# Second attention of a two-layer trunk: one pass over interleaved branches, or two passes with the compressed branch inside the first

## The reference

```python
s = einsum('bqghd,bngd->bghqn', qi, ck) * scale + tab[bucket]      # compressed: 63 keys
p_c = softmax(s) * any_valid
o_c = einsum(p_c, cv);  imp = einsum('bghqn,nm->bgqm', p_c, ov)    # importance of 16 blocks
_, idx = top_k(score(imp), 8)                                      # per group and query
o_s = softmax(q . k_selected + bias, causal) . v_selected          # selected blocks
o_w = softmax(q . k_window + bias, last 512 positions) . v_window  # local window
o = gate0 * o_c + gate1 * o_s + gate2 * o_w
```

## Time and profile before

| | us |
|---|---|
| median of the runs (3) | 2638.21 (2634.61 to 2641.0) |
| profiled execution, first to last instruction | 2632.5 |
| PE busy | 2527.8 (96%) |
| DVE busy | 1782.6 (68%) |
| ACT busy | 1124.6 (43%) |
| POOL busy | 1160.8 (44%) |
| mean granted clock of PE | 0.979 of full |

### The profile page before, as it was taken

How to read it: one execution, slowest core, us unless ns; L and a number is a source line. 1 busy time by engine, 2 the same in 40 slices (tenths; PEclk the granted TensorE clock), 3 DMA queues, 4 the chain that set the end, 5 groups by cost and what they waited for, 6 DMA issues and landing times. The chain is left out here.

```text
span 2632.5 us, 37842 instructions
## 1 busy us (share of the span) xinstructions
PE 2527.8 (96%) x14000; PEld 2051.9 (78%) x14000; DVE 1782.6 (68%) x2832; ACT 1124.6 (43%) x2184; POOL 1160.8 (44%) x883
## 2 busy tenths in 40 slices
PE   8999899999998999999988999999999999999999
PEld 5778667888887778887876788888788888777887
DVE  6544755477677999853049566666646767799993
ACT  4626543253334434323135566666524333433431
POOL 5462666244443444442236444444633444434441
PEclk8999999999999999999987799999999999999999
DMA  4110002224343544230332413122132334354531
GB/s 167 33 48 33 1 1 116 92 84 156 148 160 136 184 163 153 81 128 32 101 111 72 128 53 105 54 53 54 57 125 77 147 135 171 107 208 148 173 128 64
DMA packets 90973, 275.76 MB, mean 105 GB/s; under 512 B 9879, under 2 KB 38935, under 8 KB 76135
## 3 DMA queue, kind: packets, MB, share of 16 engines
q1 hardware_dynamic: 87240, 255.18, 28.3%
q10 hardware_dynamic: 3552, 18.18, 1.8%
HBM read 197.50 MB, written 73.86 MB: 103 GB/s over the span
## 5 line engine op out<-in xcount | busy, mean ns | idle before, releaser
L1560 PE MATMUL ps<-U_hi,RH 128*128 128x512 f32 x912 | 358.3, 393 | 19.1 <-DVE HOB L856 11.6
L1564 PE MATMUL ps<-U_lo,RH 128*128 128x512 f32 x912 | 356.8, 391 | 0.0
L1565 PE MATMUL ps<-U_hi,RL 128*128 128x512 f32 x912 | 356.7, 391 | 0.0
L1027 POOL TENSOR_TENSOR RL<-RAW,RH 128x512 fp32r<-128x512 f32 x112 | 153.5, 1371 | 419.8 <-ACT RH L737 419.8
L737 ACT ACTIVATE RH<-RAW 128x512 fp32r<-128x512 f32 x280 | 175.5, 628 | 282.9 <-PE ps L1565 275.3
L1511 POOL TENSOR_SCALAR PX<-PX,rinv,GATE 128x640 f32<-128x640 f32 (+7 forms) x256 | 197.8, 783 | 209.3 <-DVE rinv L3281 209.3
L1560 PE MATMUL ps<-U_hi,W_hi 128*128 128x512 f32 (+2 forms) x656 | 261.6, 399 | 14.1 <-DVE U_lo L2783 11.5
L1560 PE MATMUL ps<-SH,RH 128*128 128x512 f32 x656 | 255.9, 390 | 7.1 <-DVE H L896 3.2
L1564 PE MATMUL ps<-U_lo,W_hi 128*128 128x512 f32 (+2 forms) x656 | 257.8, 393 | 0.0
L1565 PE MATMUL ps<-U_hi,W_lo 128*128 128x512 f32 (+2 forms) x656 | 257.7, 393 | 0.0
L1565 PE MATMUL ps<-SH,RL 128*128 128x512 f32 x656 | 255.3, 389 | 0.0
(11 more groups left out here) (388 smaller groups left out, 5988.6 us busy)
## 6 DMA issues: line engine op xcount, KB each, us to landing
W_raw<-in_pieces SPq DMA_DIRECT2D x30, 1024.0 KB, 5.2
RAW<-in_pieces SPq DMA_DIRECT2D x28, 1024.0 KB, 4.9
RAW<-in_pieces SPq DMA_DIRECT2D x56, 512.0 KB, 7.8
hid_d<-HOA SPq DMA_DIRECT2D x24, 1024.0 KB, 3.9
hid_d<-HOB SPq DMA_DIRECT2D x24, 768.0 KB, 5.4
RHA<-hid_d SPq DMA_DIRECT2D x12, 1024.0 KB, 5.2
RHB<-hid_d SPq DMA_DIRECT2D x12, 768.0 KB, 6.7
U_rawh<-hid_d SPq DMA_DIRECT2D x12, 768.0 KB, 4.6
```

Of the source, the lines that this page charges most:

```text
L1027: G_.tensor_tensor(ring(RL[i], n), quarter(n, (B22, B11)[i - 5]), ring(RH[i], n).bitcast(F32), ALU.subtract).then_inc(u_lop.sem, 1)
L1560: m = mm(o, a_hi, b_hi, start=first, stop=False, skip_group_check=again)
L1564: mm(o, a_hi, b_lo, start=False, stop=False, skip_group_check=again)
L1565: return mm(o, a_lo, b_hi, start=False, stop=last, skip_group_check=again)
```

## The change

The 16 steps of a head pair are no longer mixed. There are 16 phases of 8 steps: eight with the window branch (one for each head pair), then eight with the selected branch (`PHASES`). The compressed branch of a head pair becomes one extra step, `CMP`, in the list of all steps `GS`: two such steps in phase 0, one in each of phases 1 to 6, none in phase 7. In phases 1 to 6 the order by key blocks is 5, 5, 5, CMP, 5, 4, 3, 2, 1; in phase 0 it is 5, 5, 5, CMP, 5, 4, CMP, 3, 2, 1; a phase of the second half is 8, 7, 6, 5, 4, 3, 2, 1. The pieces of the compressed branch are hung on the steps before and after it by fixed distances (`at_step`): scores and `turn_q` two steps ahead of it, `cmp_norm` one step ahead and at it, `add_up`, `gate_p` and `cmp_turn` one to four steps behind, `cmp_weigh` into the next phase's weighing. `cmp_scores` now uses the PSUM banks of the even unit and `turn_q` those of the odd one, so the window step behind it waits for both (`slot_free`). The row extreme is subtracted in ACT's exponential for all heads (eight instructions a head), not on POOL for every second one. The chunks of all turnings share two banks in one sequence (`X_SEQ`). The probability tile `PC` now lies in room of the raw keys (`pc`), the high and low queries in tiles `TQH` and `TQL` of their own. Turned keys of the selected branch are saved to memory and read back before the second half, and the queries are read twice, once for each branch; the window keys and first queries are turned first. The separate compressed stage is gone. The unit steps, their operations and sizes stay as they are.

```diff
-        SEL, WIN = 0, 1
-        STEPS = [x for k in range(NT) for x in ((SEL, NT - 1 - k), (WIN, NT - 1 - k))]
-        N_S = len(STEPS)
-        N_U = 2 * N_S
-        N_STEP = NH // 2 * N_S
+        SEL, WIN, CMP = 0, 1, 2
+        N_Q = NH // 2
+        PHASES = [(q, WIN) for q in range(N_Q)] + [(q, SEL) for q in range(N_Q)]
+        N_PH = 2 * NT
+        GS = []
+        for k, (q, br) in enumerate(PHASES):
+            part = [(br, k, NT - 1 - j) for j in range(NT)]
+            if k == 0:
+                part[3:3] = [(CMP, k, 0)]
+                part[6:6] = [(CMP, k, 1)]
+            elif k < N_Q - 1:
+                part[3:3] = [(CMP, k, k + 1)]
+            GS += part
+        N_G = len(GS)
+        A_OF = [sum(x[0] != CMP for x in GS[:s]) for s in range(N_G + 1)]
+        A_STEP = [x for x in GS if x[0] != CMP]
+        N_STEP = len(A_STEP)
         N_ALL = 2 * N_STEP
+        C_AT = {x[2]: s for s, x in enumerate(GS) if x[0] == CMP}
...
+        def at_step(d, g=0):
+            return {C_AT[q] + d: q for q in (range(N_Q) if not g else (3, 7))}
+        CMP_TURN = {**{s: 2 * q for s, q in at_step(3).items()}, **{s: 2 * q + 1 for s, q in at_step(4).items()}}
+        IMP_TURN, IMP_SUM, IMP_MASK = ({s: q // 4 for s, q in at_step(d, 1).items()} for d in (6, 7, 12))
...
+            load_win_bias(0)
+            load_win_bias(1)
+            save_q(0)
+            sp.wait_ge(c_mm, 2)
+            load_q(0)
+            sp.wait_ge(k_lo, 8)
+            sp.wait_ge(k_cp, 8)
+            nc.sync.dma_start(ks_d[0], KSS[:].bitcast(F32)).then_inc(k_sv[0], 16)
+            nc.sync.dma_start(ks_d[1], KS2[:].bitcast(F32)).then_inc(k_sv[1], 16)
+            save_q(1)
+            load_q(1)
+            for k in range(N_Q):
+                if k + 2 < N_Q:
+                    save_q(k + 2)
+                    load_q(k + 2)
+                    load_win_bias(k + 2)
+                if k == 3:
                     save_mask(0)
+                if k == 5:
+                    sp.wait_ge(t_tr, N_Q)
                     sp.wait_ge(i_sv, 16)
-                    for k in range(2):
-                        sp.wait_ge(t_sv[k], 32 * 6)
-                    sp.wait_ge(k_zero, 2)
-                    load_q(0)
-                    load_q(1)
-            sp.wait_ge(e_qk, NH)
-            for k in range(2):
-                sp.wait_ge(t_sv[k], 32 * (NH // 2))
-            sp.wait_ge(q_zero, 1)
-            load_q(2)
-            load_q(3)
-            sp.wait_ge(e_add, NH)
-            load_bias(2)
-            load_bias(3)
+                    sp.wait_ge(k_sv[0], 16)
+                    sp.wait_ge(k_sv[1], 16)
+                    nc.sync.dma_start(KSS[:].bitcast(F32), ks_d[0]).then_inc(ki_in, 16)
+                    nc.sync.dma_start(KS2[0:DK].bitcast(F32), ks_d[1, 0:DK]).then_inc(ki_in, 16)
+                    nc.sync.dma_start(KS2[DK + NSEL:P].bitcast(F32), ks_d[1, DK + NSEL:P]).then_inc(ki_in, 16)
+                    sp.wait_ge(ki_in, 16)
+                    nc.sync.dma_start(KS2[DK:DK + NSEL].bitcast(F32), blk_d[:, :, :]).then_inc(ki_in, 16)
+            sp.wait_ge(e_qk, NH - 2)
+            load_q(N_Q)
+            load_sel_bias(N_Q)
             save_mask(1)
             sp.wait_ge(i_sv, 32)
+            load_q(N_Q + 1)
+            sp.wait_ge(e_add, NH)
+            load_sel_bias(N_Q + 1)
+            sp.wait_ge(e_pv, NH)
...
+            STAGE = at_step(0)
+            ADD = {**{s: 2 * q for s, q in at_step(1).items()}, **{s: 2 * q + 1 for s, q in at_step(3).items()}}
+            GATE_P = {**{s: 2 * q for s, q in at_step(2).items()}, **{s: 2 * q + 1 for s, q in at_step(4).items()}}
+            for s in range(N_G):
+                for U in () if is_cmp(s) else (2 * A_OF[s], 2 * A_OF[s] + 1):
+                    hd, br, i, k0, nb = unit(U)
+                    p, c = PX[U % 7][:, 0:nb * P], U % 8
+                    pool.wait_ge(x_ri, U // 2 + 1)
+                    nc.gpsimd.tensor_scalar(p, p, rinv[:, c:c + 1], GATE[:, i, hd * 3 + 1 + br:hd * 3 + 2 + br],
+                                            ALU.mult, ALU.mult).then_inc(x_nm, 1)
+                    if U == N_ALL - N_PH - 1:
+                        pool.wait_ge(x_qk, N_ALL - N_PH)
+                        split_high(0, P_OUT1)
+                    if U == N_ALL - N_PH + 3:
+                        split_low(0, P_OUT1)
+                    if U == N_ALL - N_PH + 9:
+                        split_high(0, P_OUT1 + 1)
+                if s in STAGE and STAGE[s] + 2 < N_Q:
+                    stage_q(STAGE[s] + 2)
+                if s in ADD:
+                    add_up(ADD[s])
+                if s in GATE_P:
+                    gate_p(GATE_P[s])
...
+            def slot_free(s, e):
+                if s == 0:
+                    return
+                kind, k, x = GS[s - 1]
+                if kind != CMP:
+                    pe.wait_ge(x_max, 2 * A_OF[s - 1] + e + 1)
+                elif e == 0:
+                    pe.wait_ge(e_add, 2 * x + 2)
+                elif x + 1 < N_Q:
+                    pe.wait_ge(t_hi, x + 2)
+                    pe.wait_ge(t_lo, x + 2)
...
                 else:
+                    slot_free(s - 1, e)
...
+            def step_scores(s):
+                if is_cmp(s):
+                    q = GS[s][2]
+                    slot_free(s, 0)
+                    cmp_scores(q)
+                    if q + 1 < N_Q:
+                        slot_free(s, 1)
+                        turn_q(q + 1)
+                else:
+                    for e in range(2):
+                        slot_free(s, e)
+                        scores(2 * A_OF[s] + e)
...
+            for s in range(N_G):
+                if s + 2 < N_G:
+                    step_scores(s + 2)
+                if not is_cmp(s):
+                    a = A_OF[s]
+                    br, k, i = GS[s]
+                    turn_p(2 * a)
+                    if a:
+                        weigh_p(a - 1)
+                    if k == 0 and i == 0:
+                        cmp_weigh(0, 1)
+                        cmp_weigh(0, 0)
+                    turn_p(2 * a + 1)
+                if s in CMP_TURN:
+                    cmp_turn(CMP_TURN[s])
+                if s in IMP_TURN:
+                    imp_turn(IMP_TURN[s])
+                if s in IMP_SUM:
+                    imp_sum(IMP_SUM[s])
+                if s in IMP_MASK:
+                    imp_mask(IMP_MASK[s])
+            weigh_p(N_STEP - 1)
...
+            CMP_NORM = {**{s: 2 * q for s, q in at_step(-1).items()}, **{s: 2 * q + 1 for s, q in at_step(0).items()}}
+            CHOOSE = {s + d: (q // 4, d) for s, q in at_step(7, 1).items() for d in range(4)}
...
+            for s in range(N_G + 1):
+                after = GS[s + 2] if s + 2 < N_G else None
+                if after and after[0] == CMP:
+                    cmp_bias(2 * after[2])
+                elif after:
+                    bias(2 * A_OF[s + 2])
+                if s + 1 < N_G and not is_cmp(s + 1):
+                    inverse(A_OF[s + 1])
+                if after and after[0] != CMP:
+                    bias(2 * A_OF[s + 2] + 1)
+                if s < N_G and not is_cmp(s):
+                    copy_p(2 * A_OF[s] + 1)
+                if after and after[0] == CMP:
+                    cmp_bias(2 * after[2] + 1)
+                    if after[2] + 1 < N_Q:
+                        q_low(after[2] + 1)
+                if s in CMP_NORM:
+                    cmp_norm(CMP_NORM[s])
+                if s in CHOOSE:
+                    choose(*CHOOSE[s])
+                if s == N_G:
+                    put_out(2 * N_Q - 1, 0)
+                elif GS[s][1] >= N_Q:
+                    kind, k, i = GS[s]
+                    if i == 3:
+                        put_out(k, 1)
+                    if i == NT - 1 and k > N_Q:
+                        put_out(k - 1, 0)
```

More of the change, by code:

```diff
@@ new lines, in build_program @@
+        IMP_TURN, IMP_SUM, IMP_MASK = ({s: q // 4 for s, q in at_step(d, 1).items()} for d in (6, 7, 12))
+        X_SEQ = []
+        for s_ in range(N_G):
+            if not is_cmp(s_):
+                for U_ in (2 * A_OF[s_], 2 * A_OF[s_] + 1):
+                    X_SEQ += [("prob", U_, j) for j in range(1 + (unit(U_)[4] > 4))]
+            X_SEQ += [("cmp", CMP_TURN[s_], j) for j in range(2) if s_ in CMP_TURN]
+            X_SEQ += [("imp", IMP_TURN[s_], j) for j in range(2) if s_ in IMP_TURN]
+            X_SEQ += [("sum", IMP_SUM[s_], 0) for j in range(1) if s_ in IMP_SUM]
+            X_SEQ += [("mask", IMP_MASK[s_], j) for j in range(2) if s_ in IMP_MASK]
@@ new lines, in build_program, with copied, chunk_list, last_chunk @@
+        X_NO = {x: n for n, x in enumerate(X_SEQ)}
+        X_BY = [x[1] % 2 if x[0] == "prob" else int(x[0] == "sum") for x in X_SEQ]
+        X_COUNT = [sum(b == X_BY[n] for b in X_BY[:n + 1]) for n in range(len(X_SEQ))]
+        def copied(n):
+            return (x_cpa, x_cpv)[X_BY[n]], X_COUNT[n]
```

(44 more changed lines are left out.)

788 lines of the change are left out of this document (343 added, 445 removed).

## The result

The changed kernel takes 2684.18 us, the median of 4 runs (2680.45 to 2688.11), against 2636.62 before in the same job (4 runs): ratio 1.0176, 95% interval 1.0161 to 1.0192. It is slower by 47.6 us; forecast was 2660, slower by 21.6. The sign and most of the steps held, but the forecast was less than half of what came.

A forecast was written before the change was run, and what follows sets the result against it. TensorE was taken to bound the unit stage, VectorE the middle of the compressed stage. -118.2 + 62.4 + 9 + 58.4 + 10 = +21.6 us, so 2638.2 becomes 2660; own range 2644 to 2680, wide range 2606 to 2692.

The forecast's parts named there:

- Given back, 118.2: Start of the unit stage: first turning at 1365.0 instead of 1483.2, 118.2 us earlier; 3 less if the query load came late.
- Added work, 62.4 + 9: TensorE in the window phases: 7.8 us of compressed work per head pair, times 8, plus 9 us for the importance work.
- Waits, 58.4: TensorE's waits around each CMP step: 7.3 us a step, 58.4 in all, bounds 22 and 80.
- (a): Next even scores wait for the odd head's compressed bias, behind VectorE's copy of the odd unit: 1.6 us a CMP step.
- (b): TensorE's odd scores wait while VectorE does the extreme and the low queries: 1.15 us a CMP step.
- (c): TensorE waits for the four-block unit's bias, queued on VectorE behind the even head's cmp_norm: 3.15 us a CMP step.
- (d): TensorE waits for the three-block bias behind the odd head's cmp_norm, slowed by GpSimd's add_up: 1.4 us a CMP step.
- Clock, 10: TensorE's clock drops after waits around CMP steps: 1.25 us a step, 10 in all, bounds 0 and 3 a step.
- Split into phases, 0: Same 256 units in unmixed window and selected phases: nothing charged, with +-0.5 us a phase; selected phases 27 to 28 us.
- VectorE catches up: Rival: behind CMP steps (c) and (d) vanish and the clock holds; -25 us, 2613; chance 0.26.
- Clock low: Rival: clock stays low through much of the window phases, costing 57 us in place of 10; 2707; chance 0.10.
- Port rule in full: Fourth rival: GpSimd's scaling of two tiles also holds cmp_norm, extra 2.4 in place of 1.4; +8 us, 2668; chance 0.10.

The follow-up runs named there:

- the run with two products: Kernel with cmp_norm later and compressed biases first, leaving out one of three products per compressed score tile: 2632.1 us, 0.9979 of the kernel before.
- with the holes filled: Changed kernel plus 144 products whose result nobody uses, 6 before and 12 behind each CMP step: 2675.4 us, 1.0142 of the kernel before.
- the best kernel: Both reorderings, odd exponentials later, half the first query loads from ScalarE, cmp_norm split, GpSimd's steps spread: 2630.6 us, 0.9976 of the kernel before.
- add later: Changed kernel with GpSimd's add_up of the even head one step later: 2678.7 us, 1.0161 of the kernel before.
- the kernel with both reorderings: Changed kernel with cmp_norm behind the next biases, and compressed biases and low queries ahead of the odd unit's copy: 2638.7 us, 1.0008 of the kernel before.
- the first three runs: Changed kernel with cmp_norm one step later (2663.7 us), with compressed biases and low queries ahead of the odd copy (2659.6), and with both edits (2638.7).

## Why the prediction came out as it did

- **Given back, 118.2.** The first turning came at 1376.05; less the 8.05 us by which this execution was late, that is 1368.0, 115.2 earlier than before and 3.0 later than forecast. TensorE waited 3.99 for the query load. The text had named this as its "3 us less".
- **Added work, 62.4 + 9.** Held for the score products, by the run with two products. The rest of it wasn't taken out in any run.
- **Waits, 58.4.** In the window phases TensorE was idle 57.5 us in all. (a), (b) and (c) were right within 0.1 us each in the phase shown; `KV` and `TQL` make 17.7 in total against 22, `nmx` 24.5 against 36.4 for (c) and (d). (d) did not come, since TensorE was at half speed there. (a) to (d) thus came to 42.2 of 58.4, and small waits that the forecast had not counted, most of them at chunk banks (`PT`, `PTC`), filled the gap: that the total fits is partly luck.
- **Clock, 10.** This is the step that failed in size: "A drop doubles some 3 to 6 us of products, of which part falls into waits that are there anyway. ... I take 1.25, 10 in all". The products cost 28.6 us more than with the holes filled (26.7 more than in the best kernel). The forecast's ends were 0 and 24. After the load wait, and twice in most phases, came 3 us at 0.50 or twice that: mostly once behind (a) and (b), 1.5 and 1.1 us close together, as at 1580, and once behind the 3 us of (c), as at 1590. That each such stretch lies on the path, because TensorE has to catch up just then, is argued. Nor does the same wait always bring it: behind waits of 1.53 and 1.13 the changed kernel ran at 0.50, behind 1.53 and 1.14 "add later" ran at 1.00 (27 products in 2 us instead of 13):

```profile
1622.00:1624.00 2.00, 2.00 (x13) 1.67 (x14) 0.83 (x2) 0.64 (x2) 0.00 (x0) 0.50 1.01 250
```

```profile
1614.00:1616.00 2.00, 2.00 (x27) 1.79 (x24) 0.50 (x3) 2.00 (x6) 0.00 (x0) 1.00 1.00 246
```

- **Split into phases, 0.** Right: selected phases are 28 us, and the kernel with both reorderings has them too (219.7 us for the eight).
- **Phase 7** was forecast at 23 to 24 us and took 35.05. It holds two parts of the importance work, `choose` and the last compressed weighing, and at 1702 to 1706 it runs at 0.57 and 0.58. In the sum most of this stood elsewhere; as a mark it was wrong. So was the period of 38 to 40 us with a CMP step: the two shown took 44.7 and 42.1.
- **Sum.** The window part was forecast at 324.4 us (184.6 of unit work, taken from the 408.6 us of unit stage before less eight selected phases of 28; 71.4 added; 58.4; 10) and took 350.05: 25.7 more. With 3.0 at the start and -4.3 in the selected phases that makes the 24.4 beyond the forecast's 21.6. The clock term's 17 to 19 are the main part of it. The rest is busy time that no run assigns: added work priced too low, or more of the slow clock.
- **Chances.** The list adds up to 0.60 slower and 0.31 faster, not 0.59 and 0.32.
- **Rivals.** "VectorE catches up" was right as to what decides, and wrong for this order: moving two groups of instructions made it true, and then the break-even came (2638.7), not 2613. "Clock low" (57 us, 2707) had the right mechanism at about twice its size; its own sign, a clock under 0.8 over the window phases, did not show (0.90). "Port rule in full": the extra on the odd head's scaling is 0.94 (1.62 less 0.68), and 0.23 on the small product ahead of it; together 1.2, near the 1.4 taken and far from 2.4.

The Trainium skill, "SBUF — State Buffer", section "SBUF: two separate sides", says that a VectorE instruction with two SBUF inputs and a GpSimd one that reads SBUF exclude each other on their shared ports. The traces agree as to the exclusion (1.62 beside `add_up`, 0.68 alone), and the small product beside the scaling of units (0.40 for 0.17) shows that the scaling holds VectorE too, as rival 4 assumed. It cost little because no wide VectorE instruction with two SBUF inputs stood there. What it costs depends on who is queued behind, as the two runs with `add_up` moved show: idle time unchanged in the one, 2.8 us more in the other.

## What to carry to other kernels

When work of one stage is placed between the steps of another, go through the order of each in-order queue at that place, and put nothing longer than the consumer's cover ahead of what the bound engine needs next: here two reorderings without any change of work were worth 45 us. Count a wait of 3 us on TensorE at more than its length, for the slow products behind it; in the first three runs here a us of idle time went together with 0.7 to 0.9 us of busy time. When waits become small and equal, removing one only renames it; the measure is then TensorE's idle and busy time over a stretch with equal instruction counts, not a row of the waits.

## What the runs showed of the hardware

- TensorE's granted clock fell to 0.50 inside dense work behind waits of about 3 us, and behind waits of 1.5 and 1.1 close together, for about 3 us or twice that; behind the same 1.5 and 1.1 it also stayed at 1.00. In the kernel with both reorderings it fell at 1592 with no wait above 0.9 in the 8 us before. In the stretch compared, removing 26 us of waits (after to both) went with 18.7 us less busy time for the same 4655 products.
- Products that nobody reads made the kernel faster: 40.4 us of them, 8.8 us less in all.
- VectorE's 128x504 product of two SBUF tiles took 0.68 alone and 1.62 when GpSimd's 128x504 addition (1.16) ran beside it; moving the addition moved the delay to the next wide instruction (683 to 909 ns on average).
- Executions of unchanged code ahead of the change differed by 8 us (1115.0 to 1123.1 for the same product), over the profiles of all thirteen kernels; without a shared starting point that would have been put down to the change.
